# An attention, FFN and expert-routing kernel on one core: VectorE's weight splits between a pair's shift and its normalisation, the roots of heads placed elsewhere, forget logits in split form, another order of expert loads

## The reference, cut to what matters

```python
for l in range(2):
    ada = silu(c) @ w_ada[l] + b_ada[l]              # six rows of 1024: sh1, sc1, g1, sh2, sc2, g2
    h = x * (1 + sc1) + sh1
    y = mixer_ab(h) if l == 0 else mixer_cd(h)       # attention, then @ w_o[l]
    x = layer_norm(a * x + (1 + g1) * y)
    h = x * (1 + sc2) + sh2
    x = layer_norm(a * x + (1 + g2) * (silu(g) * u) @ w_ffn_out[l])   # g, u = h @ w_ffn_in[l]
# mixer_ab: 4 differential heads (2 softmax maps each), whose output is
#           oa * rsqrt(mean(oa^2) + eps), and 8 dilated heads
# mixer_cd: 8 MoBA heads and 8 forgetting heads; log_f = log_sigmoid(h @ w_fd + forget_b),
#           w_fd is 1024 x 8, and the bias of a score is cumsum(log_f)[q] - cumsum(log_f)[k]
# second block: conv and RG-LRU mixer, router, 32 experts of width 512:
y = (silu(xb @ w1[e]) * (xb @ w3[e])) @ w2[e]
# a gated per-layer embedding and a last norm
```

## Time and profile before

| what | value |
|---|---|
| median of three runs | 1289.89 us (1289.61 to 1289.95) |
| the profiled execution's own time | 1292.36 us |
| its span in the profile | 1290.6 us |
| mean granted clock of TensorE | 0.988 |
| PE, DVE, ACT, POOL busy | 94%, 52%, 39%, 4% of the span |
| bytes moved, mean rate | 396 MB, 307 GB/s |
| chain that ended last, by engine | PE 69%, DMA 13%, DVE 10%, ACT 5%, issue 3% |
| layer 0, its attention | about 40 to 160 us; layer 1's about 385 to 480 us |
| the experts | about 820 to 1250 us |

### The profile page before, as it was taken

One profiled execution on the slowest core, in us unless ns is written; L12 is line 12 of the kernel. 1 busy time (PEld: TensorE's weight loads), 2 busy tenths in 40 slices (PEclk: granted clock), 3 DMA queues, 4 the chain that ended last, 5 costly groups with the idle time before them and its releaser, 6 DMA issues.

```text
span 1290.6 us, 16606 instructions
## 1 busy us (share of the span) xinstructions
PE 1218.3 (94%) x6616; PEld 838.6 (65%) x6616; DVE 668.8 (52%) x1193; ACT 501.0 (39%) x744; POOL 54.8 (4%) x102
## 2 busy tenths in 40 slices
PE   6987889999999899999999999999999999999987
PEld 2686678788778877787887877544454444454436
DVE  5587968688766886774558566111111111111117
ACT  2446673343473657433445275111111111111135
POOL 0111000000000000001000300000000000000000
PEclk9998999999999999999999999999999999999999
DMA  9987667988555545777555768999999999999991
GB/s 371 391 287 226 245 240 292 271 333 322 209 190 210 208 169 216 259 264 197 193 194 204 249 245 350 394 426 427 426 427 427 394 427 427 426 427 426 425 421 41
DMA packets 48747, 396.02 MB, mean 307 GB/s; under 512 B 6225, under 2 KB 7441, under 8 KB 10418
## 3 DMA queue, kind: packets, MB, share of 16 engines
q1 hardware_dynamic: 38322, 337.69, 66.5%
q0 software_dynamic: 9568, 56.55, 12.8%
q10 hardware_dynamic: 800, 0.99, 0.2%
HBM read 391.72 MB, written 3.49 MB: 306 GB/s over the span
## 4 chain that ended last, share of the span: by engine, by line
PE 69%; DMA 13%; DVE 10%; ACT 5%; issue 3%; SPq 0%; POOL 0%; DVEq 0%; ACTq 0%
PE psum L1263 16%; PE psum L708 9%; PE psum L715 8%; PE psum L711 8%; PE psum L1302 7%; DMA slabs<-in_w 5%; DMA w_raw<-in_units 5%; PE psum L1207 4%; PE psum L1215 3%; DVE w_parts L1931 3%; DVE aring L1914 2%; DMA staged<-in_ada 2%; ACT w_parts L1389 1%; PE psum L994 1%; PE psum L1006 1%
## 5 line engine op out<-in xcount | busy, mean ns | idle before, releaser
L1931 DVE TENSOR_TENSOR w_parts<-w_raw,w_parts 128x2048 fp32r<-128x2048 f32 x106 | 242.1, 2288 | 103.1 <-ACT w_parts L1389 103.1
L1389 ACT ACTIVATE w_parts<-w_raw 128x2048 fp32r<-128x2048 f32 x106 | 202.0, 1911 | 101.2 <-DMA w_raw<-in_units 101.2
L1263 PE MATMUL psum<-slabs,arena 128*64 128x512 f32 x896 | 223.3, 593 | 4.5 <-issue 4.0
L708 PE MATMUL psum<-w_parts,h_parts 128*128 128x512 f32 x416 | 165.5, 398 | 7.6 <-DVE act_tm L2124 4.7
L711 PE MATMUL psum<-w_parts,h_parts 128*128 128x512 f32 x416 | 162.8, 391 | 0.0
L1263 PEld LDWEIGHTS psum<-slabs,arena 128*64 128x64 f32 x896 | 73.4, 137 | 113.9 <-issue 111.3
L1389 ACT ACTIVATE arena<-psum 128x512 f32<-128x512 f32 (+1 forms) x59 | 33.4, 567 | 274.7 <-PE psum L1275 141.3
L715 PE MATMUL psum<-w_parts,h_parts 128*128 128x512 f32 x416 | 112.3, 392 | 0.0
L1914 DVE CUSTOM_DVE_ANT_0 aring<-aring,cb 128x1024 f32<-128x1024 f32 x80 | 94.5, 1218 | 2.7 <-DMA aring<-in_ada 2.7
L708 PEld LDWEIGHTS psum<-w_parts,h_parts 128*128 128x128 f32 x416 | 78.4, 189 | 26.1 <-DVE act_tm L2124 6.0
L715 PEld LDWEIGHTS psum<-w_parts,h_parts 128*128 128x128 f32 x416 | 78.6, 189 | 16.8
(11 more groups left out here) (310 smaller groups left out, 1815.6 us busy)
## 6 DMA issues: line engine op xcount, KB each, us to landing
w_raw<-in_units SPq DMA_DIRECT2D x110, 1024.0 KB, 5.2
slabs<-in_w SPq DMA_DIRECT2D x32, 2048.0 KB, 18.9
slabs<-in_w SPq DMA_DIRECT2D x48, 1024.0 KB, 17.2
aring<-in_ada POOLq DMA_DIRECT2D x40, 1024.0 KB, 5.7
arena<-in_w SPq DMA_DIRECT2D x16, 2048.0 KB, 20.4
w_odd<-in_w SPq DMA_DIRECT2D x16, 2048.0 KB, 22.5
w_odd<-in_w SPq DMA_DIRECT2D x16, 1024.0 KB, 21.8
staged<-in_ada SPq DMA_DIRECT2D x8, 1024.0 KB, 16.2
```

The costliest lines, as they stand in the source:

```text
L708: mm(psum[:, bank, :], high(tile, tok), w_hi(k)[:, col:col + 512], start=first and bank not in begun, stop=False, skip_group_check=True)
L1263: ins = nc.tensor.matmul(psum[s * CAP:(s + 1) * CAP, w, :], xe_t[:, kt, s * CAP:(s + 1) * CAP], up_weights(w, s, b, kt), start=kt == 0, st ...
L1389: return nc.scalar.activation(out_ap, in_ap, func, **kw)
L1931: v.tensor_tensor(w_lo(k), raw(k), w_hi(k).bitcast(F32), ALU.subtract).then_inc(w_split, 1)
```

## The change

1. **DVE.** `split(QK_AT + 4 + pair)` stands inside `beat`, between the shift and the normalisation of that pair; before, a split stood after the normalisation and the piece. It holds for both layers. In pair 3 of layer 0 `piece(12)` stands ahead of the normalisation too, with `gate_col(0)` and `scale_heads(0)` behind it. `scale_heads(1)` follows pair 5's piece. The last split of a w_o unit stands ahead of the last normalisations in layer 1 as well.
2. **ACT.** `head_deviation(0)` stands ahead of the exponentials of pair 3 instead of behind them, `head_deviation(1)` behind the last copy of queries and keys instead of ahead of it.
3. **Forget logits.** ACT and DVE split `w_forget` once during the FFN of layer 0 (two instructions of 128x64), and PE makes 24 matmuls of fp32r operands in place of 16 of float32.
4. **SP.** One half of w3(1, 0) is issued behind the last unit of w_out. PE signals once more in the middle of the first w1 products (`up1_half`), at which SP issues the first halves of w1(1, 1) and w1(2, 0). At the end of the part that is written out, pair 8 is issued with both its w2 loads directly behind w1(8, 0), and pairs 8 and 9 are written out; the loop starts with pair 10. What is computed stays the same, and so does the number of bytes.

```diff
         w_forget = kept("w_forget", [P, KT, 8])
+        w_forget_hi = kept("w_forget_hi", [P, KT, 8], F32R)
+        w_forget_lo = kept("w_forget_lo", [P, KT, 8], F32R)
         ada = kept("ada", [P, DEPTH, 48])
...
         fd_act, fd_head = sem("fd_act"), sem("fd_head")
+        forget_split, forget_split_from = staged_in[4], 16
...
         w1_loaded = [sem("w1_loaded0"), sem("w1_loaded1")]
+        w1_begun, w1_begun_from = staged_in[6], 16
+        up1_half, up1_half_from = staged_in[7], 16
...
+            def load_w1_half(p, s, b, i, signal):
+                cols = slice(i * UNIT, (i + 1) * UNIT)
+                sp.dma_start(slab(0, s, b)[:, cols], a["w1"][p, s][:, cols]).then_inc(signal, 16)
+
+            def load_w3_half(p, s, b, i):
+                dst = w3_odd[i][:] if b and not s else slab(1, s, b)[:, i * UNIT:(i + 1) * UNIT]
+                sp.dma_start(dst, a["w3"][p, s][:, i * UNIT:(i + 1) * UNIT]).then_inc(w3_half[b][i], 16)
+
             def load_w3(p, s, b):
                 for i in range(2):
-                    dst = w3_odd[i][:] if b and not s else slab(1, s, b)[:, i * UNIT:(i + 1) * UNIT]
-                    sp.dma_start(dst, a["w3"][p, s][:, i * UNIT:(i + 1) * UNIT]).then_inc(w3_half[b][i], 16)
+                    load_w3_half(p, s, b, i)
...
             load_unit(WOUT_AT + 3)
+            sp.wait_ge(e_out, 16)
+            load_w3_half(1, 0, 1, 0)
             sp.wait_ge(unit_done, WOUT_AT + 2)
...
-            sp.wait_ge(e_out, 16)
             sp.wait_ge(normed, 20)
             sp.wait_ge(ms_sum, 6)
-            load_w3(1, 0, 1)
+            load_w3_half(1, 0, 1, 1)
...
+            sp.wait_ge(up1_half, up1_half_from + 1)
+            load_w1_half(1, 1, 1, 0, w1_begun)
+            load_w1_half(2, 0, 0, 0, w1_begun)
             for n in range(1, AHEAD):
...
                 sp.wait_ge(up1, n)
-                load_w1(n, 1, b)
-                load_w1(n + 1, 0, 1 - b)
+                if n == 1:
+                    load_w1_half(1, 1, 1, 1, w1_loaded[1])
+                    load_w1_half(2, 0, 0, 1, w1_loaded[0])
+                else:
+                    load_w1(n, 1, b)
+                    load_w1(n + 1, 0, 1 - b)
                 sp.wait_ge(up3, n)
...
             load_ups(AHEAD, AHEAD, AHEAD % 2)
-            with sp.Fori((AHEAD + 1) // 2, PAIRS // 2) as i:
+            n = AHEAD + 1
+            load_w1(n, 0, 0)
+            for c in range(2):
+                sp.wait_ge(y_mm[c], AHEAD)
+                load_w2(n, 0, c)
+            sp.wait_ge(up1, n)
+            load_w1(n, 1, 0)
+            load_w3(n, 0, 0)
+            sp.wait_ge(up3, n)
+            load_w3(n, 1, 0)
+            load_pair(n + 1, n + 1, 1)
+            with sp.Fori(n // 2 + 1, PAIRS // 2) as i:
                 for b in range(2):
...
-                    pe.wait_ge(later_in, LATER)
-                    for part in (h_hi, h_lo):
+                    pe.wait_ge(forget_split, forget_split_from + 2)
+                    for n, (w, part) in enumerate(((w_forget_hi, h_hi), (w_forget_lo, h_hi), (w_forget_hi, h_lo))):
                         for kt in range(KT):
-                            ins = mm(psum[0:8, 4, 0:T], w_forget[:, kt, :], part[:, kt, :].bitcast(F32),
-                                     start=kt == 0 and part is h_hi, stop=kt == KT - 1 and part is h_lo)
+                            ins = mm(psum[0:8, 4, 0:T], w[:, kt, :], part[:, kt, :], start=n == 0 and kt == 0,
+                                     stop=n == 2 and kt == KT - 1)
                     ins.then_inc(rows_mm, 1)
...
             rounds = pe.value_load(rounds_i[0:1, 0:1], min_val=1, max_val=4)
-            def pair(m, b, turn, last=False):
+            def pair(m, b, turn, first=False, last=False):
...
                                                    start=kt == 0, stop=kt == KT - 1)
+                        if first and w == 0 and kt == 3:
+                            ins.then_inc(up1_half, 1)
                     ins.then_inc((up1, up3)[w], 1)
...
-            pair(1, 0, 1)
+            pair(1, 0, 1, first=True)
             second_products(0, 16)
+            pe.wait_ge(w1_begun, w1_begun_from + 32)
             with pe.Fori(0, rounds * (PAIRS // 2) - 1) as i:
...
             n_all = rounds * PAIRS
-            pair(n_all, 1, rounds * (PAIRS // 2), True)
+            pair(n_all, 1, rounds * (PAIRS // 2), last=True)
             second_products(1, rounds * (PAIRS // 2 * 16))
...
                         take_pair(1, pair - 2)
+                if layer == 0 and pair == 3:
+                    head_deviation(0)
                 exps(layer, 2 * pair)
...
                 exps(layer, 2 * pair + 1)
-                if layer == 0 and pair in (3, 5):
-                    head_deviation(pair // 4)
                 if layer == 0 and pair == 4:
...
                     take_qk(layer, j)
+                    if layer == 0 and j == 7:
+                        head_deviation(1)
                     split(u + QK_AT + j + 3)
...
                     split(k + 5)
+                    if layer == 0 and g == 4:
+                        act.wait_ge(later_in, LATER)
+                        A(w_forget_hi[:], w_forget[:], Cp).then_inc(forget_split, 1)
                     gate(layer, g, 0)
...
                     pair_low(1, pair - 2)
+                split(LAYER_UNITS * layer + QK_AT + 4 + pair)
+                if layer == 0 and pair == 3:
+                    piece(9 + pair)
                 for i in items_of(layer, pair):
...
                 for j in range(2):
-                    split(u + QK_AT + j + 3)
+                    if j == 0:
+                        split(u + QK_AT + 3)
                     if layer == 1:
...
                         heads_low(0)
-                    if layer == 0 or pair:
-                        piece((9, 37)[layer] + pair)
                     if layer == 0 and pair == 3:
                         gate_col(0)
-                    if layer == 0 and pair in (3, 5):
-                        scale_heads(pair // 4)
-                    if layer or pair < 5:
-                        split(u + QK_AT + 2 + pair + 3)
+                        scale_heads(0)
+                    elif layer == 0 or pair:
+                        piece((9, 37)[layer] + pair)
+                    if layer == 0 and pair == 5:
+                        scale_heads(1)
                     if layer == 1 and pair < 3:
...
                     heads_low(1)
-                    split(u + WO_AT + 2)
+                split(u + WO_AT + 2)
                 normalise(layer, item[12])
...
                         forget_constants((g - 5) // 2)
+                    if layer == 0 and g == 5:
+                        dve.wait_ge(forget_split, forget_split_from + 1)
+                        v.tensor_tensor(w_forget_lo[:], w_forget[:], w_forget_hi[:].bitcast(F32),
+                                        ALU.subtract).then_inc(forget_split, 1)
                     if layer == 0 and at_ == 24:
```

## The result

The changed kernel takes 1271.53 us, the median of four runs (1266.22 to 1272.84); the kernel before, beside it, 1289.75 (1289.48 to 1289.95). The ratio is 0.9851, with a 95% interval of 0.9823 to 0.9879: 18.2 us faster. The profiled execution's own time was 1271.24, its span 1269.4, its mean clock 0.988. The forecast was 1267.5, in a range of 1261 to 1277.

A forecast was written before the change was run, and what follows sets the result against it. DVE bounds layer 0's attention, PE layer 1's, DMA the experts. 6.8 (layer 0) + 9.6 (layer 1) + 6.0 (experts) = 22.4 us off the median of 1289.89 gives 1267.5 us, range 1261 to 1277.

The forecast's parts named there:

- The experts' term: Expert loads: moved bytes of w3(1, 0) and two closed gaps take 6.0 us off, bounds 2.5 to 7.4.
- DVE in layer 0: Layer 0's attention: moved splits fill DVE's waits, beats become 7.6 us; 6.8 us gained, between 3.3 and 9.9.
- ahead of the write no beat waits for a piece: Layer 0's attention: before the gate column's write no beat waits for a piece's load, said against the ring's case.
- the later waits of 3.3 us: Layer 0's attention from pair 4 on: waits of 3.3 us could go too, but were not counted.
- Forget logits: Layer 1's attention: forget matmuls go from 7.00 to 2.9 us; 4.1 us gained, bounds 3.2 and 4.1.
- Layer 1's waits and clock: Layer 1's attention: of PE's waits of 4.8 us, 4.0 go, and the clock gives back 1.5 us.
- the sum of 7.4: Experts: 2.5 us for moved w3(1, 0) bytes, 2.4 for the gap at 810 to 820, 2.5 for 1008 to 1016.
- the prediction's own list of signs: Changed trace: first gap at 420 GB/s or more, last w3 read 6 us earlier, no 0.8 clock where it was 1.0.
- the ring's case: Layer 0's attention: DVE waits for late piece loads, gain only 1 to 3 us; 1272 to 1279, chance 0.24.
- That the experts give less: Expert loads: gaps reopen at later pairs, the stage gives 1 to 3 us; 1270.5 to 1273, chance 0.10.
- The slower case: Attention: thirteen moved splits wait for ACT's high part and hold up DVE; at 2.2 us each 1294, chance 0.03.
- The rule on transfer sizes: Expert loads: splitting two w1 loads into four halves costs 2.4 us of the 6.0; 1269.9, chance 0.03.

The follow-up runs named there:

- e11: Changed kernel with the half of w3(1, 0) at its old place, 16 instead of 24 router fillers and the gate column's write later: 1270.93 us.
- e8: Changed kernel with 16 instead of 24 filler matmuls of zeros in the router: 1269.09 us, ratio 0.9848.
- e10: Changed kernel with the half of w3(1, 0) at its old place and 16 instead of 24 router fillers: 1270.00 us.
- e5: Changed kernel with the half of w3(1, 0) back at its old place, all else as changed: 1271.01 us.
- e6: Changed kernel with pair 8 again issued inside the loop, its w2 loads last: 1271.03 us.

## Why the prediction was right, and which terms were off

The direction, the mechanism in attention and the range held (1271.53 in 1261 to 1277). The experts' term did not, and that the time still came out 4.0 us from the forecast owes something to luck: 3.7 us came in the two FFNs, for which nothing was forecast. By its own terms:

1. **DVE in layer 0, forecast 6.8 us.** Measured at the end of that attention 7.5 us in the first profile; over the eleven profiles with this part in them it ended at 151.9 to 155.8, median 153.7, against 159.1 to 159.5 without it, so 5.4 to 5.9 us at the median. The beat of 7.6 us came as 7.56, pair 2's shift at 81.46 instead of 81.3, the write at 97.97 instead of near 97. One step was wrong in its reason: "ahead of the write no beat waits for a piece". With beats of 7.56 us the ring is late before the write, 0.87 us in beat 3. The step that kept the later waits of 3.3 us out of the sum was right in size; they went, but PE's 4.3 us for the scaled heads, 2.0 before, and DVE's 2.6 us for scores came in their place. The clock doesn't explain the gain: this stretch lost 8.5 us to it in all three profiles with the old attention and mostly 3.4 to 5.1 with the new one, but 8.5 again in e11's, which ended at 154.0 all the same.
2. **Forget logits, forecast 4.1.** 7.00 to 2.80 us on the chain, 4.4 at the end of the attention. The 0.12 us of a product with 128 rows held for one with 8: 2.80/24 = 0.117.
3. **Layer 1's waits and clock, forecast 4.0 + 1.5.** 5.7 alone and with the forget logits 10.1 (forecast 9.6). PE's waits went from 5.2 us to 1.1, and the clock in this stretch was 1.00 throughout, where before it had cost 1.7.
4. **Experts, forecast 6.0.** This is the term that failed. Alone it gave 2.7 in the time and 2.2 in the distance; in the changed kernel's three profiles the distance fell by 3.7, 2.6 and 2.1 (424.27 to 420.60, 421.72, 422.21), and over the whole way from the convolution by 1.4, -0.3 and 2.3. The step was the sum of 7.4: it took 2.5 us for the moved half **and** 2.4 us for the gap of 810 to 820, as though they were apart. They are one budget. The half that is sent earlier leaves the queue empty sooner, ahead of the same signal of PE, which costs 2.6 to 2.7 us of hole for 2.5 us of transfer (e8 against e10 and e5, e6 against e11). The new signal closed the gap only where the half is back in place and the router is short: 0.6 us in e11 (17.4), but 2.1 and 2.2 in e10 and e5 (18.9), as much as the 2.2 of before (17.8). The third piece, 2.5 us for the gap where the loop is entered, went from 2.5 to nothing in the rate, but e6, without it, is no slower. The shorter distances are mostly bytes that moved in front of the first w1 products, by the early half and by a longer router: 424.27 - 2.5 - 3.2 + 2.0 (Empty, 6.8 less 4.8) = 420.6 for the first profile, and the same sum comes within 0.9 us of all twelve others. So the distance from the convolution, which has the router in it, is the one to judge by.
5. **The clock, forecast nothing but the 1.5 of layer 1.** In the changed kernel's three profiles the router took 21.0, 21.0 and 19.4 us against 17.8 in the four with the old loads; at 1.2 GHz the 32 products with `w_route` took 5.85 us where those of before took 3.57, and the fillers 0.43 us each where PE at 2.4 GHz takes 0.23. Another 1.6 us went in the tail of one profile, with a clock of 0.59 in 1236 to 1240. A later signal of PE made the hole in the queue larger by about as much. By the prediction's own list of signs, the low clock in stretches that had 1.0, a rate far under 420 GB/s at the first gap and 3.7 us in place of 6 at the last w3 all spoke against it.
6. **From the profiled execution to the median.** The sum was 22.4 us, and the two first profiles are 21.1 us apart in their own times (1292.36 and 1271.24). By place: 0.7 more than forecast in layer 0's attention, 1.9 and 1.8 in the two FFNs for which nothing was forecast (the first is the 1.7 us that the clock took there before and not after; in the second the chain of before has a unit's transfer of 13.89 us at 591.58 that the other has not), 0.5 in layer 1's attention, 4.6 less in convolution, router and experts, 1.6 less in the tail; 22.4 + 0.7 + 1.9 + 1.8 + 0.5 - 4.6 - 1.6 = 21.1. The other 2.9 us between 21.1 and the 18.2 of the medians come from the profiled execution of before, which was 2.6 us above its median, while that of the changed kernel was 0.3 us below its own. The forecast took the sum off the median as though both stood alike.

The rivals: the ring's case (1272 to 1279) came in its mechanism. Over the whole attention (66 to 155 us) DVE waited 0.8 to 4.1 us for `aring` in the eleven profiles with the moved splits and 0.6 to 1.1 in the three without. It took 1 us off the forecast term and not 4 to 6; its upper end of 1279 isn't covered by its own terms either (5.8 us less in layer 0 and 1.5 for layer 1's clock make 1274.8). That the experts give less is the rival that did come (forecast at 0.10). Its reason, gaps that reopen later, is a part of it (1.4 to 2.6 us from 12 to 40 us behind the first w1 products); the other part is the half's transfer counted beside the gap. The slower case didn't appear: the moved splits wait for ACT's high part 2.7 us once in layer 0 and 4.7 us in two of layer 1, and PE does not wait for them. Two of its figures were off. The earlier trace rows begin at 408 us, and from 385 us on the same wait was 8.2 us in four, the longest 2.5; and thirteen waits of 2.2 us on top of 1267.5 are 1296, not 1294.

The rule on transfer sizes of the Trainium skill ("DMA: Bandwidth & Descriptors", section Bandwidth) was put at 2.4 us. The page's 341 GB/s is for transfers issued from GpSimd, and the experts' loads are issued by SyncE. By the trace the stream of halves behind the hole ran at 425 GB/s (798 to 804), which speaks against the rule for a queue that is filled, but 4 us windows of 350 and 328 GB/s follow in the first 40 us. No run here isolates the four halves of w1.

## What to carry to other kernels

An instruction that can be done at any time belongs where its engine waits for another, and its gain can be read ahead: the wait it covers, up to the point where the next wait (here a ring of two slots, then a consumer's order) takes over. A load sent ahead of a queue that later runs dry was worth nothing by itself here: look at what the queue waits for when it is empty, and count the moved bytes or the closed gap, not both. Compare kernels by distances between the same pieces of work in the chain, and take several profiles of one kernel before a difference of two microseconds is given a cause.
